# Five token tiles in place of six in a one-core transformer layer

## The reference, cut to what matters

```python
proj = x @ w_in                                   # q, k, v and u = (GLU value, GLU gate)
q, k = _partial_rotary(q, pos), _partial_rotary(k, pos)
attn = sliding-window attention with sinks: a chunk of 64 sees itself and the chunk before
c = silu(layer_norm(causal_dwconv(u_value * sigmoid(u_gate), 31 taps)))
h = layer_norm(ALPHA * x + concat(attn, c) @ w_out)
upc = causal_dwconv(h @ w_up, 3 taps)
f = (silu(upc[..., :D_FF]) * upc[..., D_FF:]) @ w_down
ple = sigmoid(h @ w_pg + b_pg) * (p @ w_pe)
y = layer_norm(ALPHA * h + f + ple)
```

## Time and profile before

| | |
|---|---|
| median of 3 runs | 2429.86 us (2427.18 to 2430.31) |
| the profiled execution | 2428.79 us, span 2427.0 us |
| TensorE matmul busy | 2366.9 us, 98% of the span, 15081 instructions |
| GpSimd, VectorE, ScalarE busy | 66%, 61%, 53% |
| mean granted TensorE clock | 0.992 |
| moved from memory | 341.54 MB, mean 141 GB/s |

### The profile page before, as it was taken

How to read it: one execution, slowest core, us unless ns; L and a number is a source line. 1 busy time by engine, 2 the same in 40 slices (tenths; PEclk the granted TensorE clock), 3 DMA queues, 4 the chain that set the end, 5 groups by cost and what they waited for, 6 DMA issues and landing times.

```text
span 2427.0 us, 38843 instructions
## 1 busy us (share of the span) xinstructions
PE 2366.9 (98%) x15081; PEld 2329.7 (96%) x15081; DVE 1471.9 (61%) x2381; ACT 1277.3 (53%) x2086; POOL 1602.9 (66%) x1284
## 2 busy tenths in 40 slices
PE   7999999999999999999999999999999999999997
PEld 7898999999999999999999999999999999999997
DVE  6757882567766267776535767663576755374432
ACT  4557654565444456644444664445475444466653
POOL 8476887765665776566577656557775665777874
PEclk9999999999999999999999999999999999999999
DMA  6244445433333443333344433334443333535443
GB/s 239 98 150 151 163 166 174 159 135 124 122 122 105 169 158 140 124 118 122 110 166 156 148 114 118 126 114 158 153 157 122 121 122 106 174 130 183 165 146 102
DMA packets 119094, 341.54 MB, mean 141 GB/s; under 512 B 15360, under 2 KB 43648, under 8 KB 118912
## 3 DMA queue, kind: packets, MB, share of 16 engines
q1 hardware_dynamic: 98256, 312.89, 37.4%
q10 hardware_dynamic: 20656, 26.17, 3.3%
HBM read 330.12 MB, written 8.99 MB: 140 GB/s over the span
## 4 chain that ended last, share of the span: by engine, by line
PE 87%; DVE 5%; ACT 3%; POOL 2%; DMA 1%; issue 1%; DVEq 0%; ACTq 0%
PE ps L594 28%; PE ps L596 28%; PE ps L595 28%; POOL w_lo L541 2%; DVE sq L1309 1%; DMA w_raw<-in_panels 1%; ACT w_hi L771 1%; PE ps L684 1%; DVE acc L1246 1%; PE ps L672 1%; PE ps L653 1%; PE ps L662 1%; DVE u_out L1174 0%; PE ps L699 0%; DVE u_out L1172 0%
## 5 line engine op out<-in xcount | busy, mean ns | idle before, releaser
L541 POOL TENSOR_TENSOR w_lo<-w_raw,w_hi 128x512 fp32r<-128x512 f32 (+1 forms) x1272 | 1602.0, 1286 | 794.4 <-ACT w_hi L771 788.5
L771 ACT CAST w_hi<-w_raw 128x1024 fp32r<-128x1024 f32 (+2 forms) x635 | 621.8, 982 | 596.1 <-PE ps L596 404.8
L594 PE MATMUL ps<-h_hi,w_hi 128*128 128x386 f32 (+5 forms) x2496 | 814.8, 326 | 4.2 <-POOL w_lo L541 3.3
L595 PE MATMUL ps<-h_lo,w_hi 128*128 128x386 f32 (+5 forms) x2496 | 806.7, 323 | 0.0
L596 PE MATMUL ps<-h_hi,w_lo 128*128 128x386 f32 (+5 forms) x2496 | 806.6, 323 | 0.0
L594 PEld LDWEIGHTS ps<-h_hi,w_hi 128*128 128x128 f32 x2496 | 472.6, 189 | 12.1 <-issue 6.6
L595 PEld LDWEIGHTS ps<-h_lo,w_hi 128*128 128x128 f32 x2496 | 473.5, 190 | 1.3
L596 PEld LDWEIGHTS ps<-h_hi,w_lo 128*128 128x128 f32 x2496 | 473.7, 190 | 0.0
L594 PE MATMUL ps<-f_hi,w_hi 128*128 128x384 f32 (+2 forms) x1264 | 413.2, 327 | 9.6 <-issue 7.6
L596 PE MATMUL ps<-f_hi,w_lo 128*128 128x384 f32 (+2 forms) x1264 | 407.7, 323 | 0.0
L595 PE MATMUL ps<-f_lo,w_hi 128*128 128x384 f32 (+2 forms) x1264 | 407.5, 322 | 0.0
(11 more groups left out here) (153 smaller groups left out, 2008.8 us busy)
## 6 DMA issues: line engine op xcount, KB each, us to landing
w_raw<-in_panels SPq DMA_DIRECT2D x540, 512.0 KB, 3.2
w_raw<-in_panels SPq DMA_DIRECT2D x48, 384.0 KB, 2.9
w_raw<-in_panels SPq DMA_DIRECT2D x48, 128.0 KB, 2.3
xres<-in_xT ACTq DMA_DIRECT2D x32, 192.0 KB, 2.7
out_yT<-res ACTq DMA_DIRECT2D x4, 1536.0 KB, 7.3
a_raw<-in_xT ACTq DMA_DIRECT2D x6, 768.0 KB, 7.0
x_raw<-in_xT SPq DMA_DIRECT2D x2, 768.0 KB, 6.6
xres<-in_pT ACTq DMA_DIRECT2D x8, 192.0 KB, 3.4
```

The costliest lines, as they stand in the source:

```text
L541: ins = pool.tensor_tensor(w_lo[:, n % WS, c], w_raw[:, n % RS, c], w_hi[:, n % WS, c].bitcast(F32), ALU.subtract)
L594: pe.matmul(out, w_hi[:, sl, c], hi, start=first, stop=False)
L595: pe.matmul(out, w_hi[:, sl, c], lo, start=False, stop=False)
L771: act.copy(w_hi[:, n % WS, 0:w], w_raw[:, n % RS, 0:w]).then_inc(w_hi_done, 1)
```

## The change

Five tiles of 320, 448, 448, 448 and 384 tokens; with the samples the last is 418 wide. To make room, q and the rope tables have one buffer in place of two, the weights four slots in place of five, the residual input two slots (`XS`) in place of three, and the small softmax statistics lie in the squares' buffer. 320 and 448 are no multiples of 128, so attention units can hold one chunk of 64 queries: 3, 4, 4, 4 and 3 + 1 units where there were 2, 3, 3, 3, 3 and 2 + 1. The order of the head is new: tile 0's k, v and q groups come after the first four GLU groups, its attention begins within tile 0's own input groups, tile 1's input is split in two halves at the end of them, its rope table is loaded by ScalarE, 114 of the 124 taps are laid among the groups and 10 behind the attention, and four `out` groups are halved in place of five.

```diff
-LENS = [256, 384, 384, 384, 384, 256]
+LENS = [320, 448, 448, 448, 384]
-UNITS = [n // P for n in LENS[:LAST]] + [LENS[LAST] // P + 1]
+UNITS = [-(-n // P) for n in LENS[:LAST]] + [-(-LENS[LAST] // P) + 1]
-MB, WS, RS, FS, XS = 5, 5, 3, 9, 3
+MB, WS, RS, FS, XS = 5, 4, 3, 9, 2
...
-    head_taps = {1: 7, 2: 7, 3: 6, 4: 7, 5: 6, 6: 7, 7: 5, 8: 3, 9: 1, 10: 2, 11: 2, 12: 2, 13: 2}
-    for g in GLU + KVQ:
-        stage("in", 0, g)
-        first_taps(head_taps.get(g, 0))
-        if g == 7:
-            stage("x_split", 1)
-        if g == IN_V:
-            stage("x_low", 1)
-    ahead = {0: [("vt", 0)], 1: [("scores", 0, 0)], 4: [("turn", 0, 0)], 5: [("mixed", 0, 0)], 6: [("scores", 0, 1)]}
-    after = {2: [("divide", 0, 0)], 3: [("conv_add", 0, 0), ("conv_add", 0, 1)], 7: [("divide", 0, 1), ("conv_add", 0, 2)],
-             8: [("turn", 0, 1)]}
+    first = GLU[:4] + KVQ + GLU[4:]
+    head_taps = [0, 6, 7, 6, 2, 7, 2, 2, 2, 2, 7, 6, 5, 2]
+    ahead = {10: [("vt", 0)], 12: [("scores", 0, 0)]}
+    after = {11: [("x_split", 1, 0)], 12: [("x_split", 1, 1), ("x_low", 1, 0)], 13: [("x_low", 1, 1), ("divide", 0, 0)]}
+    for n, g in enumerate(first):
+        for what in ahead.get(n, ()):
+            stage(*what)
+        stage("in", 0, g)
+        for what in after.get(n, ()):
+            stage(*what)
+        first_taps(head_taps[n])
+    ahead = {1: [("turn", 0, 0)], 2: [("mixed", 0, 0)], 3: [("scores", 0, 1)], 5: [("turn", 0, 1)], 6: [("mixed", 0, 1)],
+             7: [("scores", 0, 2)]}
+    after = {1: [("table", 1)], 3: [("conv_add", 0, 0), ("conv_add", 0, 1)], 4: [("divide", 0, 1)],
+             7: [("conv_add", 0, 2)], 8: [("divide", 0, 2), ("turn", 0, 2)]}
     for n, g in enumerate(GLU + [IN_V]):
         ...
-        first_taps((9, 5, 9, 9, 11, 7, 11, 6, 0)[n])
-    stage("mixed", 0, 1)
+        first_taps((9, 8, 9, 4, 6, 9, 9, 4, 0)[n])
+    stage("mixed", 0, 2)
     stage("first_mean", 0, HB - 1)
     stage("att_split", 0)
     first_taps(1000)
...
-    stage("out_half", 4)
-HALVES = 5
+HALVES = 4
-    return min(n + (4 if n < 6 else WS if n < 8 else WS + 1), GROUPS)
+    return min(n + (WS - 1 if n < 6 else WS if n < 8 else WS + 1), GROUPS)
-    q = place("q", [2, HB, WM])
+    q = place("q", [HB, WM])
-    cos = place("cos", [2, WM])
-    sin = place("sin", [2, WM])
+    cos = place("cos", [WM])
+    sin = place("sin", [WM])
...
             def load_table(t):
-                act.wait_ge(qk_done, (t - 1) * (1 + HB))
+                act.wait_ge(qk_done, t * (1 + HB))
...
-                        parts = [(0, w, q[:, t % 2, j - 1, 0:w])]
+                        parts = [(0, w, q[:, j - 1, 0:w])]
+                        if t and j == 1:
+                            dve.wait_ge(att_done, unit_no(t, 0))
```

More of the change, by code:

```diff
@@ L354, in build @@
     prob_t = place("prob_t", [N_HEADS, P], offset=sq_base + N_HEADS * P * 4)
-    v_tok = place("v_tok", [6, P], offset=sq_base + 2 * N_HEADS * P * 4)
-    assert (2 * N_HEADS + 6) * P <= KB * WM
+    v_tok = place("v_tok", [8, P], offset=sq_base + 2 * N_HEADS * P * 4)
+    small_base = sq_base + (2 * N_HEADS + 8) * P * 4
+    smx, smax, snm, ssk, ssum, sesk, sden, sinv = (
+        place(name, [N_HEADS], offset=small_base + 32 * n)
+        for n, name in enumerate(("smx", "smax", "snm", "ssk", "ssum", "sesk", "sden", "sinv")))
+    assert (2 * N_HEADS + 8) * P + 8 * N_HEADS <= KB * WM
     par = place("par", [PARAM_COLS])
@@ L418, in computed, with last_in @@
         eng.wait_ge(pe_main, NUM[e] + 1)
+    def last_in(t):
+        return max((e for e in ORDER if e[0:2] == ("in", t)), key=NUM.get)
     def taken(eng, e):
@@ L473, in load_behind @@
                         sp.dma_start(dst, I[name]).then_inc(const_in, 16)
[L474 to L478, removed]
+                if n == RS:
+                    sp.dma_start(cos[:, 0:WIDTH[0]], I["cos"][:, 0:WIDTH[0]]).then_inc(table_in, 16)
+                    sp.dma_start(sin[:, 0:WIDTH[0]], I["sin"][:, 0:WIDTH[0]]).then_inc(table_in, 16)
                 for half, after in ((0, 6), (1, 8)):
@@ L646, in scores @@
                         if smp:
-                            mm = pe.matmul(ps[0:DEC, AUX + kv, h * P:h * P + keys], q[r, t % 2, h, SMP:SMP + DEC],
+                            mm = pe.matmul(ps[0:DEC, AUX + kv, h * P:h * P + keys], q[r, h, SMP:SMP + DEC],
                                            k_ext[r, t % 2, K_CACHE:K_CACHE + keys], start=True, stop=True)
                             continue
-                        for ab in range(2):
+                        for ab in range(rows // CHUNK):
                             none = CHUNK if first and ab == 0 else 0
@@ L667, in mixed @@
                 rows, keys, smp = unit(t, u)
-                n = DEC if smp else CHUNK
+                n = min(rows, CHUNK)
+                window = LENS[t] // CHUNK if smp else 2 * u
                 pe.wait_ge(probt_done, unit_no(t, u) + 1)
                 for kv in range(N_KV):
-                    for ab in range(1 if smp else 2):
+                    for ab in range(rows // n):
                         mm = pe.matmul(ps[HD * kv:HD * kv + HD, AUX, ab * HB * CHUNK:ab * HB * CHUNK + HB * n],
-                                       v_tok[0:keys, 2 * u + ab, HD * kv:HD * kv + HD],
+                                       v_tok[0:keys, window + ab, HD * kv:HD * kv + HD],
                                        prob_t[0:keys, HB * kv:HB * kv + HB, CHUNK * ab:CHUNK * ab + n],
@@ L1145, in take_in @@
                     own.wait()
-                    own.step(dve.tensor_tensor(src[:, 0:w], src[:, 0:w], cos[:, t % 2, 0:w], ALU.mult))
-                    own.step(dve.tensor_tensor(tmp, tmp, sin[:, t % 2, 0:w], ALU.mult))
+                    own.step(dve.tensor_tensor(src[:, 0:w], src[:, 0:w], cos[:, 0:w], ALU.mult))
+                    own.step(dve.tensor_tensor(tmp, tmp, sin[:, 0:w], ALU.mult))
                     own.wait()
```

58 lines of the change are left out of this document (29 added, 29 removed).

## The result

The changed kernel takes 2437.96 us (median of 7 runs, 2436.6 to 2438.91) against 2429.86: 1.0035 times as long (95% interval 1.0024 to 1.0047). The forecast of 2395 was wrong in sign, and the time lies outside its range. The profiled execution took 2437.28 us, its span is 2435.5 against 2427.0.

The account below looks back on a forecast made before the run. TensorE's matmuls were taken to bound the kernel, with idle time mainly in tile 0, the last tile, head and end. Terms summed to -35.1 us against 2428.8, giving 2393.7, median 2395 us; range 2371 to 2416.

Parts of the forecast that it names:

- Fixed cost per matmul: All tiles' matmuls: cost over the columns does not depend on width, so one tile fewer saves time; -30.5 us.
- rival (d): Matmuls of 418 to 450 columns cost more than their columns; gain gone at 3.7 ns each, slower from 4.3; chance 0.04.
- Stalls of tile 0: Tile 0's idle time and low clock, 22.6 us, shrink to 10 with longer groups; -13 us (bounds -22 and -5).
- the gate's block: ScalarE's convolution norm between two gates, 7.2 us at 448 columns, holds up weight casts: 3.5 us stall in tile 0.
- the waits for probabilities go: Tile 0's slots: VectorE's work grows by 1.16, slots by 1.22, so waits for softmax probabilities vanish.
- Tiles 1 to 3: The same ScalarE block against 12.1 us of cover: 0.5 us a tile, +1.5 us (0 to +12).
- Head: Start: longer input steps +1.5, tile 1's first group 0, taps between split and norm behind the attention +6 us.
- (b): Four weight slots are too few: stalls stay in tile 0 and the last tile, tiles 1 to 3 pay; 2422 us, chance 0.09.
- the end: After the last matmul groups: wider squares' sums, reciprocal, passes and store take longer; +6 us.
- the last tile's input: Where the last tile's input groups run, longer groups remove idle time and low clock; -5 us.
- attention: Sixteen full attention units become fourteen full and four half ones, beside the sample's: 55 us from 52.8, +2.2 us.
- The last tile's first slots: Longer groups remove 6.5 us of stall, but the wider ln1's stall grows by 3; -3.5 us (-8 to +3).

Follow-up runs that it names:

- The width run: A kernel without the layer, writing zeros: only groups of 24 matmuls at 22 widths up and down, then 448 and 450 without and with other engines; 202.7 ns at 448 (up).
- the last run: Changed kernel with gate split later, input splits of tiles 1 and 2 earlier, head taps moved; then tile 1's attention division ahead of tile 0's slot groups: 2407.37 us, 0.99.
- the run with room for it: Changed kernel without rope tables, values in the keys' buffer, convolution's mean using ln1's factor, and five weight slots: 2425.03 us; the same with four slots: 2440.09 us.

## Why the prediction was wrong

The forecast was -35.1 us on the profiled execution, the measured change +8.5. Four of its steps missed by 46.3 us together, a little more than the 43.6 us between forecast and measurement; others came out some 3 us better.

- **Fixed cost per matmul** (-30.5, measured -7.8: 22.7 off). The step that failed is "it does not hang on the width", drawn from 256, 290 and 384. If all of it is laid on the 9408 matmuls of 418 to 450 columns, they cost 2.4 ns each more than taken (22.7 us / 9408). This is the mechanism of rival (d), at less than the 3.7 ns from which I let it decide alone. The width run shows the same prices with nothing else at work, and that work of VectorE, ScalarE and GpSimd adds nothing. Even "13.3 at 256 and 384" was no constant: the trace of before has 12.5 and 15.8 at 290. The measured value lies outside both bounds (-45, -23): the upper one carried on the slope seen on `h`, but left `a` and `f` at 13.3. The Trainium skill (TensorE: Matmul & The Clock Gate, "Wait — 56ns, not 53.3ns?") puts the fixed cost of a warm matmul at about 2.5 ns; no width of the bench comes near it, and the least, 304, has 11.2.
- **Stalls of tile 0** (-13, measured about +2.1: 15.1 off). Idle is 18.6 us in its two windows where it was 16.5, at the same clocks. I named the gate's block and priced its wait at 3.5 us and some 2 of clock; it was 6.8 and 1.4 at the low clock behind it. The step "the waits for probabilities go" failed too: in tile 0's slots they are 4.9 us for 4.6, since they hang not on VectorE's load but on its place behind ScalarE, as the last run shows. The wait where tile 0's `d` groups meet tile 2's input, put at 4, was 3.9 and 1.6 of clock; its releaser is a weight's low part, and with the fifth slot it is gone. The 6.1 us that I added for the low clock are too many, since a low clock costs nothing while TensorE stands idle: in the changed kernel it was at 1.2 GHz from 466.3 to 473.1 us, and the gate's wait ended only at 470.1.
- **Tiles 1 to 3** (+1.5, measured 4.6: 3.1 off). The mechanism is right and its size too small: 1.3 to 1.6 us a tile. Over all tiles I priced the missing slot at 3.5 + 2 + 1.5 = 7.0 us; the run with room for it gives 15.1.
- **Head** (+7.5, measured +12.9: 5.4 off). Until ln1 of tile 0 the time grew by 36.6 us, of which 20.4 are wider matmuls and 3.3 the third attention unit. The wait at tile 1's first group was taken as 4.5 us and is 6.9; I had counted VectorE's work ahead of it and not the exponentials and the table load ahead of ScalarE's cast.
- **Right**: the end (+6, measured 2.9 behind the last matmul and 3.1 in the two norms' sums), the last tile's input (-5, measured -4.7), attention (+2.2, measured +1.9), and that the ten taps would show as a wait in the head. The last tile's first slots gave a little more than taken (-5.0 for -3.5). The end, after (VectorE, TensorE, the store), beside the earlier trace rows:

```profile
2413.70 3.83 DVE L1419 TENSOR_TENSOR res<-res,ps 128x836 f32<-128x836 f32 x4 [1.06 <-PE ps L727]
2415.71 5.88 PE L736 MATMUL ps<-sq,mean 128*128 128x418 f32 x16 [2.05 <-ACT sq L1029]
2422.24 2.78 DVE L1423 RECIPROCAL ps<-ps 128x418 f32<-128x418 f32 x1 [4.72 <-ACT ps L1032]
2428.76 2.74 SPq L522 DMA_DIRECT2D out_yT<-res  x4
```

Rows foretold as 3.85, 5.8 and 2.8 are 3.83, 5.88 and 2.78: work whose size the rows before fix was foretold well. What failed was a constant carried beyond its rows, and waits.

Behind it lies a mistake in how the cases were set. Rivals (b) and (d) stood as alternatives with 0.09 and 0.04. Both happened in part, (d) at two thirds of its threshold and (b) in tile 0 and at the gates, and neither alone would have reached "slower". A saving spread over 9408 matmuls with no row at their width deserved the larger chance. And the stalls went by mechanisms that had not been walked through on every engine: slot, ScalarE's order, VectorE's order.

The sum with what was measured: -7.8 pace, +2.1 tile 0, +4.6 gates, +12.9 head, -9.7 last tile, +1.9 attention, +6 end is +10.0 against +8.5; the rest (1.5 us) lies in terms that I did not follow singly.

**What stays open.** Why a matmul of 418 to 480 columns costs 15.5 to 20 ns over its columns, while 384 and 512 cost 13.3 to 13.5, where the steps of 6.67 ns come from, and which condition picks between 202.7 and 206.7 ns at 448. The runs show both prices, in the kernel and alone, and no cause. No run leaves out the weight load that each matmul has, or lets other engines read TensorE's results beside it, so neither is ruled out.

## What to carry to other kernels

Price a matmul at the very width that the change will use, from a row or a bench of its own; a constant found at three widths says nothing of a fourth. When tiles are widened, hand-written orders hold no longer: walk each junction engine by engine, ScalarE's table loads and casts first, and mend the order before judging the tiling (here 30.6 us lay in it, and turned a loss of 0.35% into a gain of 1%). What a look-ahead slot is worth depends on how long one group lasts: behind the gate's block TensorE waited, with four slots, 7.6 us at 256 columns, 6.8 at 320, 3.5 to 4.4 at 384 and 1.3 to 1.6 at 448.

## What of the hardware was not expected

- The time of an fp32r matmul with its own weight load is not its columns plus a constant: 173.3 ns at 384, 189.8 at 418, 202.7 at 448, 216.7 at 480, 226.9 at 512. From 480 to 512 it costs 10.2 ns for 32 columns (13.3 at 2.4 GHz), from 400 to 418 9.2 ns for 18 (7.5).
- The same width keeps to one of two prices for whole stretches: 448 columns took 202.7 ns on the way up, 206.7 on the way down, and in the kernel 202.7 in `out` of tile 1 and 206.7 in `out` of tiles 2 and 3. 290 columns took 133.3 or 136.7 in the kernel before.
- In the bench a distance that is kept throughout a stretch was a whole multiple of 6.67 ns at every width where one was kept (120.0, 146.7, 173.3, 180.0, 206.7, 220.0, 226.7); other prices are means of a short pattern that repeats.
- Work of VectorE, ScalarE and GpSimd beside it changed neither 448 (202.7 and 202.7) nor 450 (206.1 and 206.1).
- The same operation of VectorE takes very different times by where it stands: the division's first sum took 0.16 us at 317.11 in the last run and 1.16 us at 336.01 in the changed kernel, right behind the product; its long step took 1.22 us in the one and 2.02 in the other. No run tells why.
